# Mixture-of-experts blocks: token rows scattered to expert slots in memory, instead of one-hot selection products on TensorE

## The reference, cut to what matters

```
def hier_moe(x, w_grp, b_grp, w_rt, b_rt, w_gate, w_up, w_down):
    ...
    expert_id = grp_idx * MOE_EXPERTS_PER_GROUP + top_i      # two of 16 for each of 512 tokens
    gate = jnp.sum(one_hot(expert_id, MOE_EXPERTS) * top_w[..., None], axis=1)
    def step(acc, e_in):
        wg, wu, wd, ge = e_in                                # 1024x256, 1024x256, 256x1024
        hdn = jax.nn.silu(xt @ wg) * (xt @ wu)
        return acc + ge[:, None] * (hdn @ wd).astype(jnp.float32), None
```

## Time and profile before

| | us |
|---|---|
| median of 3 runs | 2656.22 (2651.23 to 2658.11) |
| profiled execution | 2656.43 |
| its span | 2654.6 |
| PE busy | 2427.4 (91%) |
| DVE, ACT, POOL busy | 1215.4, 1056.9, 827.2 |
| HBM traffic | 118 GB/s over the span |

### The profile page before, as it was taken

How to read it: one execution, slowest core, us unless ns; L and a number is a source line. 1 busy time by engine, 2 the same in 40 slices (tenths; PEclk the granted TensorE clock), 3 DMA queues, 4 the chain that set the end, 5 groups by cost and what they waited for, 6 DMA issues and landing times. The chain is left out here.

```text
span 2654.6 us, 34152 instructions
## 1 busy us (share of the span) xinstructions
PE 2427.4 (91%) x13040; PEld 1903.1 (72%) x13040; DVE 1215.4 (46%) x2393; ACT 1056.9 (40%) x1806; POOL 827.2 (31%) x281
## 2 busy tenths in 40 slices
PE   6999999779977989997996699999999899999998
PEld 5888888667746866676774557667887757677886
DVE  3655542455435448845552644363122354362123
ACT  4444342144533137734453524543223424543222
POOL 2442442324441320022434122324442322324442
PEclk9999998879988989997998799999999999999999
DMA  5126111258863331115886411313322411314212
GB/s 134 48 57 230 40 48 64 54 193 283 278 230 115 123 112 44 43 50 184 277 280 225 157 52 48 108 61 123 118 88 74 131 64 52 100 63 159 96 64 72
DMA packets 254541, 314.70 MB, mean 119 GB/s; under 512 B 55712, under 2 KB 171760, under 8 KB 254400
## 3 DMA queue, kind: packets, MB, share of 16 engines
q1 hardware_dynamic: 252096, 304.38, 36.0%
q0 software_dynamic: 2304, 8.39, 0.8%
HBM read 276.94 MB, written 35.79 MB: 118 GB/s over the span
## 5 line engine op out<-in xcount | busy, mean ns | idle before, releaser
L159 POOL TENSOR_TENSOR branch_weights_wl<-branch_weights_wf,branch_weights_wh 128x2048 fp32r<-128x2048 f32 (+1 forms) x66 | 302.0, 4577 | 770.0 <-ACT branch_weights_wh L153 770.0
L153 ACT ACTIVATE branch_weights_wh<-branch_weights_wf 128x2048 fp32r<-128x2048 f32 (+1 forms) x66 | 124.7, 1889 | 201.8 <-PE merge_acc L207 92.9
L207 PE MATMUL bmid_acc<-xh,branch_weights_wh 128*128 128x512 f32 x320 | 148.9, 465 | 9.4 <-PEq L72 9.4
L207 PE MATMUL merge_acc<-xh,branch_weights_wh 128*128 128x512 f32 x384 | 152.1, 396 | 3.4 <-PEq L72 3.4
L544 POOL TENSOR_TENSOR in_weights_wl<-in_weights_wf,in_weights_wh 128x1024 fp32r<-128x1024 f32 x32 | 79.6, 2488 | 237.6 <-ACT in_weights_wh L540 220.5
L207 PE MATMUL merge_acc<-xl,branch_weights_wh 128*128 128x512 f32 x384 | 151.9, 396 | 0.0
L207 PE MATMUL merge_acc<-xh,branch_weights_wl 128*128 128x512 f32 x384 | 151.8, 395 | 0.0
L159 POOL TENSOR_TENSOR nsa_weights_wl<-nsa_weights_wf,nsa_weights_wh 128x2048 fp32r<-128x2048 f32 x13 | 59.6, 4587 | 293.7 <-ACT nsa_weights_wh L153 293.7
L207 PE MATMUL bmid_acc<-xh,branch_weights_wl 128*128 128x512 f32 x320 | 127.3, 398 | 0.0
L207 PE MATMUL bmid_acc<-xl,branch_weights_wh 128*128 128x512 f32 x320 | 127.2, 398 | 0.0
L1754 POOL TENSOR_TENSOR rt_wl<-rt_wf,rt_wh 128x2048 fp32r<-128x2048 f32 x16 | 82.5, 5155 | 130.4 <-ACT rt_wh L1750 130.4
(11 more groups left out here) (658 smaller groups left out, 6571.2 us busy)
## 6 DMA issues: line engine op xcount, KB each, us to landing
branch_weights_wf<-w_in SPq DMA_DIRECT2D x56, 1024.0 KB, 5.1
rt_wf<-moe_w_down SPq DMA_DIRECT2D x32, 1024.0 KB, 5.6
in_weights_wf<-gdn_w_in SPq DMA_DIRECT2D x64, 256.0 KB, 3.4
rt_wf<-moe_w_gate SPq DMA_DIRECT2D x32, 512.0 KB, 7.4
rt_wf<-moe_w_up SPq DMA_DIRECT2D x32, 512.0 KB, 8.1
moe_rows<-rt_y SPq DMA_DIRECT2D x64, 256.0 KB, 2.1
moe_rows<-gdn_z SPq DMA_DIRECT2D x2, 6144.0 KB, 27.6
merge_bwf<-w_branch SPq DMA_DIRECT2D x12, 1024.0 KB, 5.0
```

The lines of the kernel that those rows point to most:

```text
L153: act.activation(self.h[u][:, :, 0:self.cols(b)], self.s.f[u][:, :, 0:self.cols(b)], ACT.Copy).then_inc(self.s.hi_ready, 1)
L159: pool.tensor_tensor(self.l[u][:, :, 0:self.cols(b)], self.s.f[u][:, :, 0:self.cols(b)], self.h[u][:, :, 0:self.cols(b)].bitcast(F32), ALU ...
L207: mm = pe.matmul(self.acc[:, s, 0:cols], lhs[:, P * s:P * s + P], rhs, start=(u == 0 and k == 0 and n == 0), stop=(u == 1 and k == HALF - ...
```

## The change

The selection is no longer computed. Instead the token rows travel through memory:

- ACT copies `g.h` to `rt.hp` with the features permuted inside each half (feature `4m+k` goes to place `128k+m`). POOL then issues eight indirect DMAs which write the rows of `hp` to their slots of `moe_rows` (each token twice, 4 MB in all). The slots that no token takes keep what they held.
- SP waits until all eight have landed and loads the rows of each block (512 KB, 4 KB a row) in one of two buffers `xr`.
- PE turns a block's rows with eight 128x128 transposes into `ps_x` (`turn_rows`); ACT makes `xh` and DVE `xl` from them for each block, in halves of 512 columns. `pick`, `choose`, `gather`, `hh` and `hl` are gone.
- Gate and up are loaded with feature `4p+k` on partition p, so each run is four rows of 256 numbers, 4 KB; in the buffer gate and up lie one behind the other (`by_matrix`), and the moving operand of a gate-and-up matmul is two runs of 256 columns.
- PE's order for block i becomes: gate and up of i, transposes of the rows of i+1, `down` of block i-1, transposes of the hidden tile of i. ACT's: `ht` of i-1, both high parts of i+1, silu of i, `x_hi` of i+1, result copies of i-1. SP's: store the result of block m, load down for m+2, then for block m+5 load unit 0, the rows, unit 1, each once its buffer is free.
- The block of tables is made right after the slots; the first two low parts of block 0 are both made by DVE.

```
             @block.sync
+                def turn_over(i, b):
+                    e = expert(i)
+                    sp.wait_ge(ws.lo_ready[0], i(1, -1))
+                    ws.load_in(sp, b, 0, e)
+                    sp.wait_ge(x_turned, i(2, -2))
+                    load_rows(b, i)
+                    sp.wait_ge(ws.lo_ready[1], i(1, -1))
+                    ws.load_in(sp, b, 1, e)
+                sp.wait_ge(sent, 16 * 2 * TT)
+                for b in range(2):
+                    load_rows(b, BlockCount(b))
...
+                with sp.Fori(0, more + 1) as j:
+                    for b in range(2):
+                        store_and_load_down(BlockCount(j * 2, b + 1), 1 - b)
+                        turn_over(BlockCount(j * 2, b + 6), b)
             @block.tensor
+                def turn_rows(b, loads, i):
+                    pe.wait_ge(x_loaded[b], loads(16))
+                    for v in range(2):
+                        if not i.is_first():
+                            pe.wait_ge(xl_out, i(2, v - 1))
+                        for k in range(HALF):
+                            col = P * (HALF * v + k)
+                            mm = pe.transpose(ps_x[:, v, P * k:P * k + P], xr[b][:, col:col + P], g.ident[:])
+                        mm.then_inc(x_turned, 1)
...
+                    if not last:
+                        turn_rows(1 - b, j.plus(b + 1), i.plus(1))
+                    if not i.is_first():
+                        down(1 - b, j.plus(b), i.plus(-1))
+                    pe.wait_ge(hid_done, i(1, 1))
...
             @block.scalar
+                def take(i):
+                    for c in range(2):
+                        act.wait_ge(y_done, i(2, c + 1))
+                        if not i.is_first():
+                            act.wait_ge(y_stored[c], i(16))
+                        act.activation(y[:, 512 * c:512 * c + 512], ps_y[:, c, :], ACT.Copy).then_inc(y_out[c], 1)
             @block.gpsimd
+                pool.wait_ge(route.slotted, 1)
+                pool.wait_ge(copied, TT)
+                for t in range(TT):
+                    for k in range(2):
+                        pool.indirect_dma_start(rows[:, :], bass.IndirectOffsetOnAxis(rt.slot_i[:, k, t:t + 1], 0),
+                                                rt.hp[:, t, :], None).then_inc(sent, 16)
     def load_in(self, sp, b, u, e):
-        for c, w in ((0, self.gate), (HID, self.up)):
+        for c, w in enumerate((self.gate, self.up)):
             src = w[bass.ds(e, 1), HALF * P * u:HALF * P * (u + 1), :]
-            sp.dma_start(self.f[b][u][:, :, c:c + HID],
-                         src.rearrange("a (k p) n -> p (a k) n", p=P)).then_inc(self.loaded[b][u], 16)
+            sp.dma_start(self.by_matrix(self.f[b][u])[:, c],
+                         src.rearrange("a (p k) n -> p (a k) n", k=HALF)).then_inc(self.loaded[b][u], 16)
```

More of the change, by code:

```diff
@@ L1820, in store, with expert @@
                                      y[:, 512 * c:512 * c + 512]).then_inc(y_stored[c], 16)
-                with sp.Fori(1, end + 1) as j:
-                    for b in range(2):
[L1824 to L1831, removed]
+                def expert(i):
+                    return sp.value_load(rt.table[0:1, bass.ds(i(), 1)], min_val=0, max_val=N_EXP - 1)
@@ L1832, in _ @@
+                last = BlockCount(more * 2, 7)
+                store_and_load_down(last.plus(-4), 1)
                 for u in range(2):
-                    sp.wait_ge(ws.lo_ready[u], end * 2 + 1)
+                    sp.wait_ge(ws.lo_ready[u], last())
                 nxt.load_first(sp)
-                for b in range(2):
-                    store(end * 2 + b)
+                store_and_load_down(last.plus(-3), 0)
+                store_and_load_down(last.plus(-2), 1)
+                store(last.plus(-1))
@@ L1837, in _ @@
+                store(last)
                 sp.wait_ge(ln_in, 16 * len(rt.loads))
@@ L1841, in _ @@
                 route.pe(pe)
[L1843 to L1860, removed]
@@ L1883, in body @@
                     mm.then_inc(t_done, 1)
[L1884 to L1889, removed]
-                        if not first(i):
-                            pe.wait_ge(y_out[c], i)
-                        for k in range(2):
-                            mm = pe.matmul(ps_y[:, c, :], ht[:, k, :], down[:, k, c, :], start=(k == 0), stop=(k == 1))
-                        mm.then_inc(y_done, 1)
-                for v in range(2):
-                    for part in range(2):
-                        gather(0, v, part)
-                pairs(pe, body)
+                turn_rows(0, BlockCount(1), BlockCount(0))
+                loads, last = pairs(pe, body)
+                down(1, loads, last)
             @block.scalar
@@ new lines, in hidden, with x_hi @@
+                def hidden(i):
+                    act.wait_ge(t_done, i(1, 1))
+                    if not i.is_first():
+                        act.wait_ge(y_done, i(2))
+                    act.activation(ht[:].rearrange("p k n -> p (k n)"), ps_t[:, 0, 0:HID], ACT.Copy).then_inc(ht_out, 1)
+                def x_hi(i):
+                    for v in range(2):
+                        act.wait_ge(x_turned, i(2, v + 1))
+                        act.activation(halves(xh)[:, v, :], ps_x[:, v, :], ACT.Copy).then_inc(xh_out, 1)
@@ L1941, in body @@
-                    if b == 1 and not last:
-                        x_hi(j + 1, 1)
-                    for c in range(2):
-                        act.wait_ge(y_done, i * 2 + (c + 1))
-                        if not first(i):
-                            act.wait_ge(y_stored[c], i * 16)
-                        act.activation(y[:, 512 * c:512 * c + 512], ps_y[:, c, :], ACT.Copy).then_inc(y_out[c], 1)
-                for u in range(2):
-                    ws.hi(act, 0, u, 1)
-                x_hi(0, 0)
@@ L1951, in _ @@
-                x_hi(0, 1)
-                pairs(act, body)
+                        x_hi(i.plus(1))
+                    else:
+                        nxt.hi_first(act)
+                        nxt.hi_second(act)
+                    if not i.is_first():
+                        take(i.plus(-1))
+                for u in range(2):
+                    ws.hi(act, 0, u, BlockCount(1))
+                x_hi(BlockCount(0))
+                _, last = pairs(act, body)
+                hidden(last)
@@ L2027, in _ @@
                 for c in range(2):
[L2028 to L2029 removed]
+                    dve.wait_ge(y_stored[c], last(16, 16))
+                dve.tensor_copy(route.mx[:, 0, :], route.tm[:, 0, :])
 CA_ROW = T + P
```

242 lines of the change are left out of this document (111 added, 131 removed).

## The result

The changed kernel took 2589.61 us (median of 4 runs, 2585.17 to 2594.05) against 2656.3 us: ratio 0.9756, 95% interval 0.9743 to 0.977. Its profiled execution took 2594.05 us with a span of 2592.1 us, 62.5 us less than the span before. The prediction said 2612 with a range of 2593 to 2642: right in direction, 22 us too high at the median and some 3 us outside the range.

A forecast was written before the change was run, and what follows sets the result against it. PE set the old pace; afterwards PE (10.1 us) and DMA (10.4) come out level, taken as 10.6 a block. Two layers save 32.6 us each, later starts cost 11.8 and 9.3: 2656.4 - 44.1 = 2612 us, 8-in-10 range 2593 to 2642.

The forecast's parts named there:

- PE, 10.1 us a block: Expert loop, PE's work per block: 13.07 us less 3.9 for gather matmuls, plus 0.9 for eight transposes, about 10.1 us.
- I take 10.6 us a block: Expert loop period, taken between 10.1 (PE alone) and 11.7 us, as two nearly full resources don't mesh perfectly.
- The price of the DMA, 404 GB/s: Expert loop: full DMA engines move a block's 4.194 MB at 404 GB/s, 10.4 us.
- Rival B: PE sets the loop at 10.1 us and the scatter gets through earlier: 14 + 6 us less, 2592 us; chance 0.14.
- The first block, "8.4" and "3.5" for the cold clock: Loop start: 8.4 us until the second block's x is there, plus 3.5 us lost to PE running at 1.2 GHz.
- The last block, 15.5: Loop end: gate-and-up 5.8 us, then the last two `down` products, with `ht` late on ACT; together 15.5 us.
- The start, +11.8 and +9.3: Stage start: scatter, landing, row load and turning make the first gate-and-up 11.8 us later in layer 0, 9.3 in layer 1.
- The ring: Loop waits through SP's list, the stores, `take`, ACT and POOL: some 17 us per two blocks against 21.2, so it holds.
- rival C: Transfers ahead of the stores slow the loop to 12.2 us a block (gain gone) or 13.1 (2682 us); chance 0.06.
- Costed at nothing: Terms priced at zero, among them ACT's four permuted copies, covered by the slots even if strided reading doubled their 4 us.
- rival D: Longer gate-and-up runs don't help, loads stay at 350 GB/s: 11.2 us a block, 2629 us; chance 0.27 together with A.
- rivals A and D: A: DMA sets the loop's pace at 11.2 to 11.7 us a block, 2629 to 2643 us; chance 0.27 including D.

## Why the prediction was off, point by point

- **PE, 10.1 us a block: right** (10.085). The doubled turn measures the eight transposes at 0.88 us against 0.9 forecast, and columns in two runs of 256 cost nothing that shows: gate-and-up matmuls start 0.23 us apart before and after.
- **The step that failed: "I take 10.6 us a block",** between 10.1 and 11.7, because two nearly full resources don't mesh perfectly. No row stood behind that allowance, and here they do mesh: 10.04 or 10.13 in every period. Half a microsecond over 14 periods is 7.2 us a layer, 14.4 of the 20.7 us by which the table's sum and the forecast differ. Two things were wrong in it. The price of the DMA, 404 GB/s, was too low: 412 to 417 with the stores among the loads. And a lag of the DMA was charged at once, where it has to pile up for five to eight blocks before PE sees it (rows loaded twice, short runs). The second alone would have been enough: with the prediction's own 10.4 us the lag over 14 blocks is some 4 us (an estimate), less than the 6 to 7 that the buffers held.
- **Rival B** came out close to the result (2592) in part by luck. Its period of 10.1 us was the right one, 14 of its 20 us, but its scatter that gets through 6 us earlier did not come; the first and the last blocks, shorter than forecast by some 6 us in all, stood in for it.
- By the rule of the Trainium skill, "DMA: Bandwidth & Descriptors", section "Where 436 GB/s comes from", that the HBM side binds such transfers at about 358 GB/s, a block would have taken 11.7 us, an estimate; the trace does not agree, with 412 to 417 over whole blocks.
- **The first block, "8.4" and "3.5" for the cold clock:** 9.85 instead of 11.9. At full clock it is 7.68, and the clock costs 2.2, not 3.5. That is 2.1 us in layer 0 (2.0 in layer 1).
- **The last block, 15.5:** 14.9, from 736.23 to 751.10. `ht` does stand behind the next stage's high parts; PE waits 1.67 us for it (1.03 in layer 1).
- **The start, +11.8 and +9.3: right** (+12.1 and +8.6), and for the reason given, bytes in a full queue: leaving out the scatter gives back 11.8 and 11.3 us, SP issues the rows at 579.36 where 577.9 + 1.4 was forecast. "Ten us for eight" on POOL missed the 5.06 us of the second; the full queue hid it.
- **The ring** over the one `y` and SP's list held: up to 4.0 us of waiting for the stores in `take`, and none in PE. With 12.5% more traffic it still held, and the DMA's rate was the bound, with periods of 11.35 to 11.60 and not the 12.2 or 13.1 of rival C.
- **Costed at nothing, and rightly:** ACT's permuted copies took 7.75 us, twice the 4 of before, and end at 554.4, ahead of the slots at 556.5. The same stride on DVE's low parts, where nothing covers it, costs 3.2 us a stage (the long runs alone).
- **The 1 KB rate of 350** for rival D was about right. With the other half of a block's bytes at 413 GB/s it gives 11.1 us, and the run with short runs showed 11.0 (381 for the mix). What failed for rivals A and D is that they need the DMA as the bound for the whole loop: even at 381 GB/s PE met it only in the later half.

## What to carry to other kernels

Here two resources that came out level cost no more than the slower of them. So price such a loop at the slower of the two and nothing on top; then work out how many blocks the buffers hold the lag, and charge only the blocks that are left. A DMA share near 1 is no measure of what is left: 357 and 417 GB/s both show it, so ask the bytes per period against the rate of a run that is known to be full. Data that is scattered to memory and read back at once costs its bytes at the start of a stage, so whatever else is in that queue and isn't wanted first should go behind it.

## What the runs showed of the hardware

- One core moved 412 to 417 GB/s between memory and SBUF for 100 us, with an eighth of it stores; with the gate and up loads in 1 KB runs, half of the bytes, 379 to 381.
- An indirect DMA's issue took 0.96 us on POOL, and 5.06 beside two DVE subtractions whose two inputs both lie in SBUF (4.47 us). In layer 1, where the subtractions begin later against the issues, it is the third one, 4.17 us; in both layers the held issue ends 0.85 or 0.86 us after the second subtraction. It went away when they were moved, in both kernels that did so. The Trainium skill, "SBUF — State Buffer", section "Who interferes with whom", has such a DVE operation contend with GpSimd's reads of SBUF; the trace agrees, and an indirect DMA's issue is among what is held up. There the section, which infers that such an operation doesn't hold up the making of DMA descriptors, and the trace differ.
- Reading every fourth f32: ACT 7.75 us for four copies of 128x1024, against 3.89 in order; DVE 8.06 for eight subtractions against 4.90.
- The stretch between the two expert stages, which no edit touched, took 416 to 424 us from one execution to the next. In the same 30 us of it, counted from the stage's end, first the changed kernel and then the one with the rows first:

```profile
904.70:934.70 30.00, 30.00 (x167) 24.28 (x166) 9.88 (x21) 6.15 (x9) 7.45 (x2) 0.89 0.38 134
```

```profile
898.70:928.70 30.00, 30.00 (x186) 24.54 (x186) 13.63 (x25) 9.83 (x13) 7.76 (x3) 1.00 0.39 132
```

PE is busy throughout in both, at a granted clock of 0.89 in the one and 1.00 in the other. Edits worth under 4 us were therefore read from stage lengths, not from medians. What lowers the clock in a busy engine stays open.
